# Adding the other experts' sums into PSUM by unit products, with a new order of the last units

## The chip, the cores and the metric

The kernel runs on one core of one Trainium2 chip. The metric is the device time of one execution in microseconds (us), the median of three runs. The engines are TensorE (PE; its weight loads are listed as PEld), VectorE (DVE), ScalarE (ACT), GpSimd (POOL) and SyncE (SP), which here only issues transfers.

## The reference

Two layers of a decoder trunk on 256 tokens of width 1024, all in f32. Each layer has a mixer (causal spatial gating beside latent attention) and a channel part. The channel part of the second layer is a top-2-of-8 mixture of SwiGLU experts, and the change lies at its end:

```python
h = rms_norm(x, norm_ffn_pre) * (1 + sc_f) + sh_f          # (256, 1024)
# for each token the two experts with the highest logits, gates = softmax of the two
y[token] = sum over its 2 experts e of gate * (silu(h @ w1[e]) * (h @ w3[e])) @ w2[e]
x = x + g_f * rms_norm(y, norm_ffn_post)                   # the output
```

Each expert has 3584 hidden columns; w1, w3 and w2 of all eight experts are 352 MB, and each is read once.

## The kernel before

**Units.** The expert stage is cut into 56 units (`UNITS`, from `SMALL_AT`): eight experts times `NG` = 7 groups of 512 hidden columns. A unit needs three pairs of weight chunks, 2 MB each (w1, w3, w2). Experts are sorted by their number of tokens. Four are *large* (up to 128 rows; each weight chunk is split by ACT and DVE into two f32r parts, and PE makes three products for each, lines 2177 to 2179). Four are *small* (64 rows, the expert `TINY` 32; PE multiplies the f32 chunk as it is, line 2692, with two or four products beside each other in the array). `SMALL_AT` says at which of the 56 places a unit of a small expert stands. The last expert is `END`, a small one: its units 3 to 6 are units 52 to 55.

**PE's order.** `unit(n)` does the w1 products of unit n, the transposes of unit n-1 (line 2734), the w3 products of unit n, and `unit_down(n-1)`, the w2 products of the unit before. After the loop come `unit_down(55)` and `last_scatter`. PE does all in this order.

**Weights.** SP issues the transfers in the order of use, into a ring of places; a transfer waits until PE has used what lay in its place. Pairs go as one transfer of 2 MB. Only the last pair, the w2 of unit 55 (`LAST_PAIR`), goes as two transfers of 1 MB with a semaphore each.

**Rows of the other experts.** When an expert other than `END` is finished (two units after its last one), ACT scales its rows by the gates and POOL writes them to a table in HBM by an indirect DMA (`scatter_rows`, line 864; its count is `rows_out`). When all are written (`ALL_ROWS`), POOL clears two buffers and gathers from the table, for each of the two blocks of 128 tokens, the first and the second choice (four indirect DMAs of 512 KB, line 896) into `y_exp` and `y_second`. DVE adds the two (line 2142).

**The end.** PE has the sums of `END` in bank 6. ACT copies them to `r5` (`last_y`, line 1338). `last_scatter` (line 2869) distributes the rows to the tokens by four products of 64 rows, one for each block t and half of the width (q = 2t + half), into the banks `DRAIN`. DVE adds each bank to `y_exp` (`add_y`, line 2025), ACT squares each half with its sum (`y_half`, line 1347), DVE and ACT make 1/rms (`y_inverse`, line 2123, and `root`, line 946), DVE multiplies by the gate row (`gated`, line 2129), scales and adds the residual (`last_residual`, line 2134), and SP stores four halves of 256 KB (line 702).

Of the kernel before, what the change touches and what calls it, by code (L numbers as in the profile page):

```python
# [223 lines left out]
def item_order():  # L224

    out = []
    for g in range(NG):
        out += [(spot(kind, g, 0), kind, g) for kind in ("w1", "w3")]
        if g:
# [3 lines left out]

LAST = [(PER_ITEM - 2, "w2", NG - 1)]
DRAIN = (7, 0, 1, 2)

LARGE = 5
HALF_CAP = P // 2
# [4 lines left out]
SMALL_ITEMS = (0, 5, TINY, 6)  # L243
LARGE_ITEMS = tuple(range(1, LARGE))
SMALL_AT = (0, 1, 2, 3, 4, 5, 6, 7, 8, 9, 11, 13, 16, 19,
            22, 25, 28, 31, 34, 37, 41, 44, 47, 49, 52, 53, 54, 55)


def units():
# [52 lines left out]
def up_width(n):  # L302
    return GRP * small_cap(UNITS[n][0]) // P
# [27 lines left out]
def build(nc, A, out):  # L331
    with ExitStack() as ctx:
# [3 lines left out]
        def sem(name):  # L336
            return ctx.enter_context(nc.semaphore(name))
# [161 lines left out]
        def raw_of(r, e=CH):  # L499
            slot = RING[r][0]  # L500
            if slot >= ONCE_AT:
                return (r3, r57)[slot - ONCE_AT][:, 0:e]
            if slot == HIDDEN_AT:
                return b_whole[1].rearrange("p k s -> p (k s)")[:, 0:e]
            if slot >= TURNED_AT:
                return hT_raw[slot - TURNED_AT][:, 0:e]
            if slot >= HIGH_AT:
                return hi_raw[:, slot - HIGH_AT, 0:e]
            return raw[:, row_of(slot), 0:e] if slot <= NRAW else r6[:, (slot - NRAW - 1) * CH:(slot - NRAW - 1) * CH + e]
# [87 lines left out]
        x0_dve = sem("x0_dve")  # L597
        ym_done, xh_done, hf_dve, hbt_full, rs_ready = (sem(n) for n in ("ym_done", "xh_done", "hf_dve", "hbt_full", "rs_ready"))
        rows_out, y_in, y_whole = sem("rows_out"), sem("y_in"), sem("y_whole")
        m_sm = sem("m_sm")  # L600
        rows_marked, y_cleared = sem("rows_marked"), sem("y_cleared")
        tiny_slots = sem("tiny_slots")
        small_ready, experts_ready, half_ready = sem("small_ready"), sem("experts_ready"), sem("half_ready")
# [8 lines left out]
        def _(sp):  # L612
# [53 lines left out]
            def moe_load(c, kind, e, g):  # L666
                src = A["moe_" + kind]
                src = src[e, g] if isinstance(e, int) else src[bass.ds(e, 1), g, :, :].rearrange("e p n -> p (e n)")
                if paired(c):
                    sp.wait_ge(used, NW + max(RING[NR + c + half][2] for half in range(2)) - NR + 1)  # L670
                    sp.dma_start(pair_of(NR + c), src).then_inc(raw_full[RING[NR + c][3]], 16)
                    return
                for half in range(2):
                    r = NR + c + half
                    slot_free(r)
                    sp.dma_start(raw_of(r), src[:, half * CH:(half + 1) * CH]).then_inc(raw_full[RING[r][3]], 16)

            expert = {0: 0}

# [16 lines left out]
            unit_loads(UNITS_ALL - 1, ("w2",))  # L696

            def store(n):
                for i, (t, half) in enumerate(((1, 0), (1, 1), (0, 0), (0, 1))):
                    sp.wait_ge(o_done, 4 * n + i + 1)  # L700
                    at = slice(half * 512, (half + 1) * 512)
                    sp.dma_start(out[0, t * P:(t + 1) * P, at], o_sb[:, t, at]).then_inc(out_done, 16)
# [14 lines left out]
        def _(pool):  # L717
# [160 lines left out]
            for n in range(UNITS_ALL):  # L878
                if n in FINISH_AT:
                    scatter_rows(FINISH_AT[n])  # L880
                if n == CLEAR_AT:
                    clear_rows(END)
                    wait_emptied(pool, LAST_IN[ONCE_AT + 1])
                    take_gate(3, gate_f, gate_f_in)
            pool.wait_ge(rows_out, ALL_ROWS)
            pool.wait_ge(m_gath, 2 * EXPERTS)
            wait_emptied(pool, LAST_IN[NRAW + 1])
            for t in range(T):
                pool.memset(y_second[t][:, :], 0.0).then_inc(y_cleared, 1)
            pool.memset(y_exp, 0.0).then_inc(y_cleared, 1)  # L890
            pool.wait_ge(rows_marked, 1)
            pool.wait_ge(y_cleared, T + 2)
            for t in range(T):
# [8 lines left out]
        def _(act):  # L902
# [443 lines left out]
            def y_half(q):  # L1346
                act.activation(scratch[:, q // 2, (q % 2) * 512:(q % 2 + 1) * 512], y_exp[:, q // 2, (q % 2) * 512:(q % 2 + 1) * 512],
                               ACT.Square, scale=D ** -0.5, accum_out=ms[:, q:q + 1]).then_inc(sq_done, 1)
# [5 lines left out]
            act.activation(warm[:, :], warm[:, :], ACT.Sqrt)  # L1354
            last_y()
            for q in range(4):
                act.wait_ge(m_acc, q + 1)
                y_half(q)
                if q % 2:
                    root(1, q // 2)  # L1360
            act.wait_ge(route_ready, 1)
# [14 lines left out]
        def _(dve):  # L1376
            steps = [0]

            def link(ins):

                steps[0] += 1
                ins.then_inc(v_step, 1)
                dve.wait_ge(v_step, steps[0])
# [635 lines left out]
            def add_y(i, q, bank=7):  # L2019

                ya = y_exp[:, q // 2, (q % 2) * 512:(q % 2 + 1) * 512]
                if q == 0 and i >= EXPERTS:
                    dve.wait_ge(m_acc, (i - (EXPERTS - 1)) * 4)
                dve.wait_ge(m_sc, (i - (EXPERTS - 1)) * 4 + q + 1)
                dve.tensor_tensor(ya, ya, ps[:, bank, :], ALU.add).then_inc(m_acc, 1)
# [102 lines left out]
            def gated(t):  # L2128
                return dve.tensor_tensor(y_sb[:, t, :], y_exp[:, t, :], gate_f[:, :], ALU.mult)
# [12 lines left out]
                dve.tensor_tensor(y_exp[:, t, :], y_exp[:, t, :], y_second[t][:, :], ALU.add).then_inc(y_whole, 1)  # L2142
            dve.wait_ge(y_whole, T)
            dve.wait_ge(gate_f_in, 16 * L)
            for q in range(3):
                add_y(EXPERTS - 1, q, DRAIN[q])
            y_inverse(0)
            add_y(EXPERTS - 1, 3, DRAIN[3])
            dve.wait_ge(m_acc, 4)
            gated(1)  # L2150
            y_inverse(1)
            link(gated(0))
            dve.wait_ge(rstd_ready, roots[0])
            last_residual(1)
            last_residual(0)
            spare = dve.value_load(info[0:1, ITEMS:ITEMS + 1], min_val=0, max_val=SPARE)
            with dve.If(spare > 0):
                dve.wait_ge(out_done, 64)
                for i in range(EXPERTS, ITEMS):
                    with dve.If(spare > i - EXPERTS):  # L2160
                        spare_item(i)
                        drain(i)
                dve.memset(small[:, 1:2], 0.0).then_inc(sum_ready, 1)
                gated(0)
                link(gated(1))
                y_inverse(0)
                y_inverse(1)
                dve.wait_ge(rstd_ready, roots[0])
                last_residual(1)
                last_residual(0)  # L2170


        @block.tensor
        def _(pe):
# [505 lines left out]
            def whole_part(c):  # L2680

                wait_full(pe, NR + c)
                return raw_of(NR + c)

            def part(i, c):
                return moe_part(i * PER_ITEM + c)

# [49 lines left out]
            def unit_down(n, turn_next=False):  # L2737
                i, g = UNITS[n]
                small = SMALL[n]
                if g == 0:  # L2740
                    before_ = same_kind_before(FINISH + [END], i)
                    if before_ is not None:
                        pe.wait_ge(m_yc, FINISHED[before_])
                    elif not small:
                        pe.wait_ge(idx_ready, 3)
                pe.wait_ge(m_h, n + 1)
                if small:
                    for half in range(2):
                        w = whole_part(unit_chunk(n, "w2", half))
                        for cc in range(2):  # L2750
                            cap, turned = small_cap(i), up_width(n) // P
                            c = 2 * half + cc
                            m = beside(6, D, cap, hT_small(n)[:, c % turned, c // turned * cap:(c // turned + 1) * cap], w, cc * D,
                                       g == 0 and c == 0, g == NG - 1 and c == 3)
                        m.then_inc(used, 1)
                        if turn_next and half == 0:
                            unit_turn(n + 1)
                    return
                for half in range(2):
                    wh, wl = moe_part(unit_chunk(n, "w2", half))  # L2760
                    for cc, q in itertools.product(range(2), range(2)):
                        c = 2 * half + cc
                        w = slice(cc * D + q * 512, cc * D + (q + 1) * 512)
                        first, final = g == 0 and c == 0, g == NG - 1 and c == 3
                        m = three(ps[:, 4 + q, :], bTh[:, c, 0:P], bTl[:, c, 0:P], wh[:, w], wl[:, w], first, final)
                    m.then_inc(used, 1)
                    if turn_next and half == 0:
                        unit_turn(n + 1)
# [95 lines left out]
            def last_scatter():  # L2864
                pe.wait_ge(m_gtc, 1)
                pe.wait_ge(m_yc, EXPERTS)
                for q in range(4):
                    at = slice(q % 2 * HALF_CAP, (q % 2 + 1) * HALF_CAP)
                    pe.matmul(ps[:, DRAIN[q], :], r4[at, 512 + q // 2 * P:512 + (q // 2 + 1) * P], r5[at, 0:512],
                              start=True, stop=True).then_inc(m_sc, 1)  # L2870

            for n in range(UNITS_ALL):
                unit(n)
            unit_down(UNITS_ALL - 1)
            last_scatter()
            pe.wait_ge(route_ready, 1)
# [94 lines left out]
```

## Time and profile before

| | |
|---|---|
| median of three runs | 1364.44 us (1363.46 to 1365.38) |
| the profiled execution | 1364.49 us |
| its span | 1362.8 us |
| outside the span | 1.69 us |
| PE busy | 1327.3 us, 97% |
| DVE, ACT busy | 903.3 us (66%), 675.1 us (50%) |
| read from HBM | 496.12 MB, 367 GB/s over the span |

Times in the text are counted from the start of the span. A row of the timeline gives the start, the duration, the engine, the line, what it writes and reads, the number of instructions merged, and in brackets the idle time before it and what ended it. Durations of PE's rows overlap, since products are pipelined; the distance between starts is what a product costs in a full queue. An f32 product stands as two records (line 2869 is four products and eight records).

### The profile page before, as it was taken

How to read it: one execution, taken by the hardware profiler on the slowest of the kernel's cores; microseconds unless marked ns; L12 is line 12 of the kernel's file. 1: busy time of each engine (PE TensorE's matmuls, PEld its weight loads, DVE VectorE, ACT ScalarE, POOL GpSimd, SP SyncE). 2: the span in 40 equal slices, each digit the busy share in tenths (PEclk: the TensorE clock that was granted, in tenths of full speed). 3: DMA queues.
4: the chain of work that ended last, by engine and by line, in shares of the span. 5: the costliest groups of instructions: out<-in, count | busy, mean ns of one | idle time of the engine just before them, and what ended most of it. 6: DMA issues, size and time to landing. Idle time of an engine off the chain costs nothing.

```text
span 1362.8 us, 19221 instructions
## 1 busy us (share of the span) xinstructions
PE 1327.3 (97%) x7925; PEld 1021.0 (75%) x7925; DVE 903.3 (66%) x1105; ACT 675.1 (50%) x773; POOL 60.0 (4%) x133
## 2 busy tenths in 40 slices
PE   9999999999999999999999999999998999999985
PEld 6788879878888888656677777777877887777752
DVE  6799979878778965200366765775767687676513
ACT  2783553534467643112355645565646576554501
POOL 6000000000000000100000000000000001000020
PEclk9999999999999999999999999999998999999998
DMA  9929939988654599899999999999999999999994
GB/s 367 418 107 351 390 111 397 422 314 347 236 203 163 194 385 407 335 421 423 425 428 427 428 428 399 428 427 427 427 428 426 427 427 427 428 427 427 427 427 192
DMA packets 52959, 500.59 MB, mean 367 GB/s; under 512 B 6272, under 2 KB 6400, under 8 KB 13058
## 3 DMA queue, kind: packets, MB, share of 16 engines
q1 hardware_dynamic: 50114, 490.90, 87.3%
q0 software_dynamic: 2752, 8.41, 1.7%
q8 instruction: 64, 1.05, 0.3%
q14 instruction: 29, 0.24, 0.0%
HBM read 496.12 MB, written 4.08 MB: 367 GB/s over the span
## 4 chain that ended last, share of the span: by engine, by line
PE 81%; DMA 9%; DVE 6%; ACT 2%; SPq 1%; issue 1%; DVEq 0%; ACTq 0%
PE ps L2177 20%; PE ps L2179 20%; PE ps L2178 19%; PE ps L2692 16%; DMA raw<-in_moe_w_dram 7%; PE ps L2671 2%; DMA raw<-in_w_first_dram 2%; PE ps L2734 1%; DVE lo L1454 1%; DVE lo L1482 1%; ACT hi L928 1%; ACT hi L911 1%; DVE raw L1395 1%; DVE mx L1688 0%; DVE r L1696 0%
## 5 line engine op out<-in xcount | busy, mean ns | idle before, releaser
L1482 DVE TENSOR_TENSOR lo<-raw,hi 128x2048 fp32r<-128x2048 f32 x136 | 308.6, 2287 | 174.7 <-ACT hi L928 174.6
L2177 PE MATMUL ps<-hi,hT_hi 128*128 128x512 f32 (+3 forms) x912 | 355.1, 389 | 4.2 <-DVE hT_lo L1508 1.9
L2179 PE MATMUL ps<-hi,hT_lo 128*128 128x512 f32 (+3 forms) x912 | 348.9, 383 | 0.0
L928 ACT ACTIVATE hi<-raw 128x2048 fp32r<-128x2048 f32 x136 | 256.0, 1913 | 158.0 <-DMA raw<-in_moe_w_dram 158.0
L2178 PE MATMUL ps<-lo,hT_hi 128*128 128x512 f32 (+3 forms) x776 | 295.6, 381 | 0.0
L2177 PEld LDWEIGHTS ps<-hi,hT_hi 128*128 128x128 f32 x912 | 171.3, 188 | 47.3 <-issue 13.0
L2179 PEld LDWEIGHTS ps<-hi,hT_lo 128*128 128x128 f32 x912 | 171.2, 188 | 32.6
L1454 DVE TENSOR_TENSOR lo<-raw,hi 128x2048 fp32r<-128x2048 f32 (+3 forms) x82 | 174.7, 2143 | 24.8 <-ACT hi L911 23.5
L2177 PE MATMUL ps<-hi,bT_hi 128*128 128x512 f32 (+2 forms) x416 | 166.0, 399 | 9.2 <-DVE bT_lo L1999 8.7
L2178 PEld LDWEIGHTS ps<-lo,hT_hi 128*128 128x128 f32 x776 | 145.8, 188 | 25.1
L2178 PE MATMUL ps<-lo,bT_hi 128*128 128x512 f32 (+2 forms) x416 | 162.6, 391 | 0.0
L2179 PE MATMUL ps<-hi,bT_lo 128*128 128x512 f32 (+2 forms) x416 | 162.3, 390 | 0.0
L911 ACT ACTIVATE hi<-raw 128x2048 fp32r<-128x2048 f32 (+3 forms) x82 | 145.3, 1802 | 30.0 <-DMA raw<-in_w_fu_dram 15.8
L2692 PE MATMUL ps<-raw,bT_first 128*32 128x128 f32 (+3 forms) x1456 | 124.6, 367 | 4.4 <-DMA raw<-in_moe_w_dram 4.4
L2692 PEld LDWEIGHTS ps<-raw,bT_first 128*32 128x32 f32 (+1 forms) x1456 | 62.0, 119 | 56.4 <-issue 41.8
L2177 PEld LDWEIGHTS ps<-hi,bT_hi 128*128 128x128 f32 (+1 forms) x416 | 79.0, 190 | 33.3 <-DVE bT_lo L1999 8.6
L1250 ACT ACTIVATE bT_first<-ps 128x256 f32<-128x256 f32 (+1 forms) x28 | 10.0, 357 | 177.0 <-PE ps L2734 177.0
L1395 DVE SCALAR_TENSOR_TENSOR raw<-raw,c_rows 128x1024 f32<-128x1024 f32 x80 | 94.6, 1219 | 0.1
L2179 PEld LDWEIGHTS ps<-hi,bT_lo 128*128 128x128 f32 (+1 forms) x416 | 79.2, 190 | 16.0
L2692 PE MATMUL ps<-raw,bT_second 128*64 128x256 f32 x752 | 87.8, 387 | 2.9 <-DMA raw<-in_moe_w_dram 2.9
L2178 PEld LDWEIGHTS ps<-lo,bT_hi 128*128 128x128 f32 (+1 forms) x416 | 79.3, 191 | 14.7
L2006 DVE TENSOR_TENSOR r<-r,ps 128x256 f32<-128x256 f32 (+1 forms) x28 | 10.7, 383 | 112.4 <-PE ps L2692 112.4
(384 smaller groups left out, 1266.3 us busy)
## 6 DMA issues: line engine op xcount, KB each, us to landing
raw<-in_moe_w_dram SPq DMA_DIRECT2D x116, 2048.0 KB, 17.2
r<-in_moe_w_dram SPq DMA_DIRECT2D x22, 2048.0 KB, 16.0
raw<-in_w_ada_dram SPq DMA_DIRECT2D x40, 1024.0 KB, 7.6
raw<-in_moe_w_dram SPq DMA_DIRECT2D x36, 1024.0 KB, 12.4
hi_raw<-in_moe_w_dram SPq DMA_DIRECT2D x13, 1024.0 KB, 11.1
raw<-in_w_fd_dram SPq DMA_DIRECT2D x11, 1024.0 KB, 8.3
raw<-in_w_ga_dram SPq DMA_DIRECT2D x8, 1024.0 KB, 6.9
raw<-in_w_gb_dram SPq DMA_DIRECT2D x8, 1024.0 KB, 6.8
```

Source lines behind the costliest of these rows:

```text
L911: act.activation(high_of(s, e), raw_of(r, e), ACT.Copy).then_inc(hi_done, 1)
L928: act.activation(high_of(s), raw_of(r), ACT.Copy).then_inc(hi_done, 1)
L1395: m = dve.scalar_tensor_tensor(w, w, 1.0, cbc[:, :], ALU.mult, ALU.mult, accum_out=av[:, k:k + 1])
L1454: dve.tensor_tensor(low_of(r, e), raw_of(r, e), high_of(s, e).bitcast(f32), ALU.subtract).then_inc(raw_done, 1)
L1482: dve.tensor_tensor(low_of(r), raw_of(r), high_of(s).bitcast(f32), ALU.subtract).then_inc(raw_done, 1)
L2006: dve.tensor_tensor(h_small[:, 0:w], h_small[:, 0:w], ps[:, 1, 0:w], ALU.mult).then_inc(m_sm, 1)
L2177: pe.matmul(o, wh, mh, start=first, stop=False)
L2178: pe.matmul(o, wh, ml, start=False, stop=False)
L2179: return pe.matmul(o, wl, mh, start=False, stop=last)
L2671: m = pe.matmul(ps[:, 3, kk * P:kk * P + width], x[:, t, k * P:(k + 1) * P], r4[:, t * P:t * P + width], start=(t == 0), stop=(t == T - 1))
L2692: m = pe.matmul(ps[q * cap:(q + 1) * cap, bank, 0:width], stationary, w[:, at + q * width:at + (q + 1) * width], start=first, stop=last)
L2734: m = pe.transpose(ps[:, 2, c * P:(c + 1) * P], src[:, c * P:(c + 1) * P], ident[:, :])
```

## The change

1. **Order of the units.** The last small places in `SMALL_AT` move: large units end at unit 49 instead of 51, so that units 46 to 49 are four large ones in a row, and units 50 to 55 are six small ones of `END`.
2. **POOL.** It no longer waits for all rows ahead of the clearing; the first buffer waits for nothing new, the second for the rows of `TINY`, and the wait for `ALL_ROWS` stands behind the clearing.
3. **Unit products.** DVE no longer adds the scattered banks to `y_exp`. Instead PE writes `y_exp` into the four banks `SUM_BANK` by products with the unit matrix `ident` (`first_sums`), between `unit(55)` and `unit_down(55)`, and `last_scatter` adds to these banks (`start=False`).
4. **The end.** ACT squares from the banks; DVE multiplies bank by gate half by half after each square, and goes through block 0 ahead of block 1.
5. **The last chunk.** Its 1 MB goes in two transfers of 512 KB; the first has a semaphore of its own (`last_half_in`), so that PE can use it ahead of the second.

```diff
+SUM_BANK = (3, 4, 5, 7)
...
 SMALL_AT = (0, 1, 2, 3, 4, 5, 6, 7, 8, 9, 11, 13, 16, 19,
-            22, 25, 28, 31, 34, 37, 41, 44, 47, 49, 52, 53, 54, 55)
+            22, 25, 28, 31, 34, 37, 41, 45, 50, 51, 52, 53, 54, 55)
...
                     slot_free(r)
-                    sp.dma_start(raw_of(r), src[:, half * CH:(half + 1) * CH]).then_inc(raw_full[RING[r][3]], 16)
+                    parts = 2 if c + half == LAST_PAIR + 1 else 1
+                    for q in range(parts):
+                        at, w = q * CH // parts, CH // parts
+                        landed = last_half_in if parts == 2 and q == 0 else raw_full[RING[r][3]]
+                        sp.dma_start(raw_of(r)[:, at:at + w], src[:, half * CH + at:half * CH + at + w]).then_inc(landed, 16)
...
-            pool.wait_ge(rows_out, ALL_ROWS)
             pool.wait_ge(m_gath, 2 * EXPERTS)
             wait_emptied(pool, LAST_IN[NRAW + 1])
             for t in range(T):
+                if t:
+                    pool.wait_ge(rows_out, ROWS_OUT[TINY])
                 pool.memset(y_second[t][:, :], 0.0).then_inc(y_cleared, 1)
             pool.memset(y_exp, 0.0).then_inc(y_cleared, 1)
+            pool.wait_ge(rows_out, ALL_ROWS)
...
             for q in range(4):
-                act.wait_ge(m_acc, q + 1)
-                y_half(q)
+                act.wait_ge(m_sc, q + 1)
+                act.activation(scratch[:, q // 2, (q % 2) * 512:(q % 2 + 1) * 512], ps[:, SUM_BANK[q], :],
+                               ACT.Square, scale=D ** -0.5, accum_out=ms[:, q:q + 1]).then_inc(sq_done, 1)
                 if q % 2:
                     root(1, q // 2)
...
-            for q in range(3):
-                add_y(EXPERTS - 1, q, DRAIN[q])
-            y_inverse(0)
-            add_y(EXPERTS - 1, 3, DRAIN[3])
-            dve.wait_ge(m_acc, 4)
-            gated(1)
-            y_inverse(1)
-            link(gated(0))
-            dve.wait_ge(rstd_ready, roots[0])
-            last_residual(1)
-            last_residual(0)
+            for t in range(T):
+                for half in range(2):
+                    q = 2 * t + half
+                    dve.wait_ge(sq_done, squares[0] + half + 1)
+                    m = dve.tensor_tensor(y_sb[:, t, half * 512:(half + 1) * 512], ps[:, SUM_BANK[q], :], gate_f[:, half * 512:(half + 1) * 512],
+                                          ALU.mult)
+                m.then_inc(y_whole, 1)
+                y_inverse(t)
+            dve.wait_ge(y_whole, 2 * T)
+            for t in range(T):
+                dve.wait_ge(rstd_ready, roots[0] - T + t + 1)
+                last_residual(t)
...
+                        last = unit_chunk(n, "w2", half) == LAST_PAIR + 1
+                        w = half_part(LAST_PAIR + 1) if last else whole_part(unit_chunk(n, "w2", half))
                         for cc in range(2):
+                            if last and cc:
+                                w = whole_part(LAST_PAIR + 1)
...
-                    pe.matmul(ps[:, DRAIN[q], :], r4[at, 512 + q // 2 * P:512 + (q // 2 + 1) * P], r5[at, 0:512],
-                              start=True, stop=True).then_inc(m_sc, 1)
+                    pe.matmul(ps[:, SUM_BANK[q], :], r4[at, 512 + q // 2 * P:512 + (q // 2 + 1) * P], r5[at, 0:512],
+                              start=False, stop=True).then_inc(m_sc, 1)
+
+            def first_sums():
+                pe.wait_ge(m_gtc, 1)
+                pe.wait_ge(m_yc, EXPERTS - 1)
+                pe.wait_ge(y_whole, T)
+                for q in range(4):
+                    pe.matmul(ps[:, SUM_BANK[q], :], ident[:, :], y_exp[:, q // 2, q % 2 * 512:(q % 2 + 1) * 512], start=True, stop=False)
 
             for n in range(UNITS_ALL):
                 unit(n)
+            first_sums()
             unit_down(UNITS_ALL - 1)
             last_scatter()
```

The order of the stores (block 0 first) and a branch that these inputs don't enter follow along.

## Rows read from the trace of the kernel before

**Rows 1.** The page: PE's busy time, share of the span, instructions.
```profile
PE 1327.3 (97%) x7925; PEld 1021.0 (75%) x7925; DVE 903.3 (66%) x1105; ACT 675.1 (50%) x773; POOL 60.0 (4%) x133
```
**Rows 2.** Stretches: PE, PEld, DVE, ACT, POOL busy; then PEclk, DMA share, GB/s.
```profile
1200.00:1300.00 100.00, 99.89 (x547) 73.05 (x546) 64.07 (x68) 47.90 (x38) 0.00 (x0) 1.00 1.01 428
...
1320.00:1337.00 17.00, 13.13 (x86) 7.45 (x84) 0.42 (x1) 0.66 (x2) 3.01 (x3) 0.90 1.00 419
1337.00:1347.00 10.00, 6.94 (x36) 2.17 (x34) 2.42 (x3) 1.87 (x3) 0.00 (x0) 1.00 0.48 199
```
**Rows 3.** Timeline of ACT: splits that waited for the next 2 MB of weights.
```profile
1191.81 3.72 ACT L928 ACTIVATE hi<-raw 128x2048 fp32r<-128x2048 f32 x2 [2.38 <-DMA raw<-in_moe_w_dram]
1196.71 3.72 ACT L928 ACTIVATE hi<-r 128x2048 fp32r<-128x2048 f32 x2 [1.18 <-DMA r<-in_moe_w_dram]
```
**Rows 4.** Timeline of PE, the last weights.
```profile
1321.90 3.65 PE L2692 MATMUL ps<-raw,bT_first 128*64 128x512 f32 x16 [1.31 <-DMA raw<-in_moe_w_dram]
...
1340.14 1.94 PE L2692 MATMUL ps<-raw,bT_first 128*64 128x512 f32 x8 [2.62 <-DMA raw<-in_moe_w_dram]
...
1342.38 3.65 PE L2692 MATMUL ps<-raw,bT_first 128*64 128x512 f32 x16
1346.47 1.94 PE L2692 MATMUL ps<-raw,bT_first 128*64 128x512 f32 x8 [0.45 <-DMA raw<-in_moe_w_dram]
```
**Rows 5.** Timeline of POOL: the last write of rows, the clearing, the first gather.
```profile
1303.66 0.96 POOL L864 DMA_INDIRECT rows_y<-r,choice_row  x1 [146.07 <-PE ps L2692]
1314.37 0.95 POOL L889 MEMSET c_rows<- 128x1024 f32 x1 [9.76 <-DMA rows_y<-r,choice_row]
...
1318.84 1.08 POOL L896 DMA_INDIRECT r<-rows_y,final_row  x1 [0.88 <-POOL r L890]
```
**Rows 6.** Timeline of DVE: the sum of both choices.
```profile
1345.01 1.23 DVE L2142 TENSOR_TENSOR r<-r,c_rows 128x1024 f32<-128x1024 f32 x1 [6.94 <-DMA gate_m<-rows_y,final_row]
```
**Rows 7.** Timeline of PE: f32 products of 512 columns, and the next row.
```profile
41.86 1.88 PE L2239 MATMUL ps<-gate_m,raw 128*128 128x512 f32 x4
43.58 2.42 PE L2239 MATMUL ps<-r,raw 128*128 128x384 f32 x8
```
**Rows 8.** Timeline of PE: f32r products of 512 columns, one record each.
```profile
1153.10 0.40 PE L2177 MATMUL ps<-hi,hT_hi 128*128 128x512 f32 x1
1153.33 0.39 PE L2178 MATMUL ps<-lo,hT_hi 128*128 128x512 f32 x1
```
**Rows 9.** Timeline: the scatter, the first sum, the first residual.
```profile
1349.26 1.99 PE L2869 MATMUL ps<-r 64*128 64x512 f32 x8 [0.85 <-ACT r L1338]
...
1350.49 1.88 DVE L2025 TENSOR_TENSOR r<-r,ps 128x512 f32<-128x512 f32 x3 [3.12 <-PE ps L2869]
...
1356.20 2.74 DVE L2134 SCALAR_TENSOR_TENSOR r<-raw,rstd,x_tok 128x512 f32<-128x512 f32 x4
```
**Rows 10.** Groups by line, 1330 to 1363 us: busy us, mean ns, idle before.
```profile
L2025 DVE TENSOR_TENSOR r<-r,ps 128x512 f32<-128x512 f32 x4 | 2.6, 680 | 3.1 <-PE ps L2869 3.1
L1347 ACT ACTIVATE r<-r 128x512 f32<-128x512 f32 x4 | 2.5, 617 | 2.1 <-DVE r L2025 2.1
...
L1347 ACT ACTIVATION_READ_ACCUMULATOR r<-r 128x1 f32 x4 | 0.7, 186 | 0.0
...
L946 ACT ACTIVATE rstd<-mean_sq 128x1 f32<-128x1 f32 x2 | 0.4, 202 | 1.1 <-DVE mean_sq L2125 1.1
...
L2125 DVE RECIPROCAL mean_sq<-mean_sq 128x1 f32<-128x1 f32 x2 | 0.3, 164 | 0.1
```
**Rows 11.** Timeline of PE: starts of units 43 (large), 44 and 46.
```profile
1152.29 0.50 PE L2177 MATMUL ps<-hi,hT_hi 128*128 128x512 f32 x1
...
1169.29 3.67 PE L2692 MATMUL ps<-raw,bT_second 128*64 128x256 f32 x32
...
1197.50 0.50 PE L2177 MATMUL ps<-hi,hT_hi 128*128 128x512 f32 x1
```
**Rows 12.** Weight transfers issued from 1100 to 1300: issue to landing.
```profile
DMA to landing us min/median/max: 12.5/17.7/19.8
```

More of the change, by code:

```diff
@@ L599, in build @@
         rows_out, y_in, y_whole = sem("rows_out"), sem("y_in"), sem("y_whole")
-        m_sm = sem("m_sm")
+        m_sm, last_half_in = sem("m_sm"), sem("last_half_in")
         rows_marked, y_cleared = sem("rows_marked"), sem("y_cleared")
@@ L698, in store @@
             def store(n):
-                for i, (t, half) in enumerate(((1, 0), (1, 1), (0, 0), (0, 1))):
+                for i, (t, half) in enumerate(((0, 0), (0, 1), (1, 0), (1, 1))):
                     sp.wait_ge(o_done, 4 * n + i + 1)
@@ L2158, in _ @@
                 dve.wait_ge(out_done, 64)
+                for q in range(4):
+                    dve.tensor_copy(y_exp[:, q // 2, (q % 2) * 512:(q % 2 + 1) * 512], ps[:, SUM_BANK[q], :]).then_inc(m_acc, 1)
                 for i in range(EXPERTS, ITEMS):
@@ L2168, in _ @@
                 dve.wait_ge(rstd_ready, roots[0])
+                last_residual(0)
                 last_residual(1)
-                last_residual(0)
         @block.tensor
@@ L2683, in whole_part, with half_part @@
                 return raw_of(NR + c)
+            def half_part(c):
+                pe.wait_ge(last_half_in, 16)
+                return raw_of(NR + c)
             def part(i, c):
@@ L2748, in unit_down @@
                     for half in range(2):
-                        w = whole_part(unit_chunk(n, "w2", half))
+                        last = unit_chunk(n, "w2", half) == LAST_PAIR + 1
+                        w = half_part(LAST_PAIR + 1) if last else whole_part(unit_chunk(n, "w2", half))
                         for cc in range(2):
+                            if last and cc:
+                                w = whole_part(LAST_PAIR + 1)
                             cap, turned = small_cap(i), up_width(n) // P
@@ L2868, in last_scatter @@
                     at = slice(q % 2 * HALF_CAP, (q % 2 + 1) * HALF_CAP)
-                    pe.matmul(ps[:, DRAIN[q], :], r4[at, 512 + q // 2 * P:512 + (q // 2 + 1) * P], r5[at, 0:512],
-                              start=True, stop=True).then_inc(m_sc, 1)
+                    pe.matmul(ps[:, SUM_BANK[q], :], r4[at, 512 + q // 2 * P:512 + (q // 2 + 1) * P], r5[at, 0:512],
[4 more added lines that the diff above has]
+                pe.wait_ge(y_whole, T)
+                for q in range(4):
+                    pe.matmul(ps[:, SUM_BANK[q], :], ident[:, :], y_exp[:, q // 2, q % 2 * 512:(q % 2 + 1) * 512], start=True, stop=False)
             for n in range(UNITS_ALL):
                 unit(n)
+            first_sums()
             unit_down(UNITS_ALL - 1)
```

## The prediction

> **What bounds the kernel now.** I read the page first: PE is busy for 97% of the span [rows 1], which says little here, since records of pipelined products overlap. The stretches say more. From 1200 to 1300 us the transfers have a DMA share of 1.01 at 428 GB/s, and still 1.00 at 419 GB/s from 1320 to 1337; only in the last ten microseconds of the stream does it fall to 0.48 [rows 2]. So the expert stage ends when the weights have come in. ACT's splits show the pace: each waited for a DMA, 4.90 us apart, which is one pair of chunks of 2 MB [rows 3]. Then I read the end of PE's timeline. The work on the last but one pair, w2 of unit 54, begins at 1340.14 after 2.62 us of waiting for it; from there PE works without a pause to 1346.03 (1342.38 + 3.65), waits only 0.45 us for the last chunk, and ends at 1348.41 [rows 4]. That is what the reader is to see: ahead of the last chunk PE has almost no spare time. From 1321.90 to 1346.47, four pairs, the pace is 6.14 us, not 4.90: the gathers run beside the weights there, from 1318.84 [rows 5] to 1345.01, where DVE's wait for the last of them ends [rows 6]. They cost the stream 24.57 - 4 x 4.90 = 4.97 us.
>
> After the last product the chain goes ACT copy, PE scatter at 1349.26, DVE add at 1350.49, squares, gate, and the first residual at 1356.20 [rows 9].
>
> **Edit 1 and 2, order and POOL.** Today POOL clears its buffers only when the last write of rows, issued at 1303.66, has landed, at 1314.37, and gathers from 1318.84 [rows 5]. With the large units done two places earlier that write comes about two units, some 29 us (six pairs of 4.90), earlier. The clearing then waits for the place of `y_exp`, which unit 52 still uses for its w3, so that the gathers begin near 1301 and land near 1327 (the 26 us that they take now, from rows 5 and 6). The bytes are the same and the transfers have no free time in which to hide them (1.01 to 1300, 1.00 to 1337 [rows 2]): the 4.97 us are paid earlier, and the end of the stream stays at 1346.47. But the last pairs then come at the undisturbed pace. w2 of unit 54 lands 4.90 ahead of the end, at 1341.57, instead of 1340.14: this step alone costs 1.43 us, as PE's work after that pair has no slack.
>
> Four large units in a row: a large unit after a large one takes 17.0 us on PE [rows 11] against 14.7 us for its three pairs, so PE falls back by 2.3 us in each. Now it begins unit 46 at 1197.50, 5.7 us after the split of its weights began at 1191.81 [rows 3, 11]; with unit 44 large and unit 45 small I make that 8, and after four large ones 15. What is late next is the issue of the transfer that takes the freed place. The worst pair, w2 of unit 48, whose products come a unit later, would be used up some 20 us after it landed; the next pair in its place is due six pairs, 29.4 us, after it, so that issue to landing falls to about 9.3 us, where the shortest now is 12.5 [rows 12]. A pair takes 4.90, so I take no gap in the stream; below I price one. The six small units then need less of PE than the weights take, and it catches up before unit 54.
>
> **Edit 3, the unit products.** Four f32 products of 512 columns on the whole array. The nearest row: two such products (four records) take 43.58 - 41.86 = 1.72 us, 0.86 each [rows 7]; four are 3.44 us. The lower bound is the price of f32r operands, 0.23 each [rows 8], 0.92 in all; the upper the row's full 1.88 for two, 3.8. `ident` and `y_exp` are f32, so I take 3.44. They stand in PE's order behind all of unit 55, `unit_down(54)` included, and ahead of `unit_down(55)`. The 2.62 us in which PE waits lie ahead of that place [rows 4] and can't cover them; behind it there are 0.45. What queues behind them is the last down product, and ACT's copy and the scatter wait for that. Their own wait for DVE's sum costs nothing: gathers that land at 1327 let DVE add in about 1341 to 1343.5, right behind its part of unit 55, while PE reaches the products near 1346.
>
> The Trainium skill, page "TensorE: Matmul & The Clock Gate", part "Wait — 56ns, not 53.3ns?", has bf16 products of 512 columns starting 215.7 ns apart. If that held here the four would be 0.86 us and the forecast 2.6 us lower; the f32 row above, four times as long, speaks against it.
>
> **Edit 5, the last chunk in two.** PE now does the chunk in 1.94 us after it lands. Alone, the split could hide half, 0.97. But PE arrives late: 1341.57 + 5.89 + 3.44 = 1350.9, when all of the chunk has lain there for 4 us. So I take 0, and 0.97 as the bound on the side of a gain.
>
> **Edit 4, the end**, counted from the start of the scatter. Now the first residual starts at 6.94 [rows 9]. After: banks ready at 1.23 as for DVE today; two squares of 0.62 and a read of 0.19 [rows 10] are done at 2.04 and 2.66; DVE multiplies (0.68 each, the add's duration) to 2.72 and 3.40; two small operations of 0.16 and their links bring 3.76; ACT, which stands in its order at the root (0.20), is free at 4.0. Squares 3 and 4 are done at 4.8 and 5.4, the products at 6.2, the small operations at 6.5, and the first residual starts: 0.45 earlier. The chain keeps its length because a read and a product of half a block now follow each square, in place of the four adds that go. Bounds: between 0 and a gain of 0.9, if records overlap as the three adds do (1.88 for three of 0.68).
>
> **The sum.** PE's work from the last but one pair: 5.89 + 1.94 = 7.83 now, 11.27 with the unit products. 1341.57 + 11.27 = 1352.84 against 1348.41: 4.43 later. Less 0.45: +3.98. The profiled execution took 1364.49 us, 0.05 over the median, so 1368.4 us.
>
> **The rivals.**
> *The pair lands as now.* If the gathers still end late, the pair keeps its 1340.14 and only the products count: 3.44 - 0.45 of idle - 0.45 = +2.5, 1367.0. For it: unit 52's use of the place. Against: 1301 is far from 1341.
> *The stream ends earlier*, the mechanism that ends on the other side: if the gathers, moved among units that PE bounds, find free transfer time, the stream loses up to 4.97 us less. Then 3.98 - 4.97 = -1.0, 1363.5; it is faster than now from 4 us on. Against it: a DMA share of 1.01 before 1300 [rows 2].
> *The unit products are covered*, as the change would have it: PE would have to wait 3.44 us for the last chunk. Then only edits 4 and 5 count, -0.97 - 0.45 = -1.4, 1363.1. Against: 0.45 us of idle.
> *The products are cheap* (0.92): +1.5, 1365.9.
> *The stream starves* in the four large units: a gap of 2 to 3 us goes straight to the end, 1371.
>
> **How the numbers follow.** Under 0.2%, 2.7 us, a difference of this kernel can't be told from none. Forecast 0.57, of which 0.05 fall under 2.7, since it lies only 1.3 above; pair as now 0.16, 0.07 of it over; early stream 0.08; covered 0.03; cheap 0.04; starved 0.08; something else that gains more than 2.7 us 0.04. Slower: 0.52 + 0.07 + 0.08 = 0.67; faster 0.04; same the other 0.29. The range leaves out the early stream, the cover and the unnamed gain, 0.15 together: it reaches from 1364.5 (cheap products, pair as now, 0.92 - 0.45 - 0.45) to 1371.4 (starved).
>
> **What would show it.** Right: eight records of `first_sums` lasting about 3.4 us between two stretches of line 2692; no idle of PE between them and the scatter beyond ACT's copy; last waits of PE for DMA 4.9 us apart; gathers issued near 1301; the scatter starting near 1353.7. Wrong: a wait of PE for weights behind the unit products, a stream that ends before 1345, or DMA share under 0.95 between 1240 and 1300.

## The result and the profile after

The changed kernel takes 1368.57 us (median of 7 runs, 1367.13 to 1369.8), beside 1364.72 us for the kernel before (7 runs): a ratio of 1.003, interval 1.002 to 1.004. The forecast was 1368.4 us, slower. The profiled execution took 1368.34 us with a span of 1366.6, which is 3.8 us over the span before. One run of the kernel before (1903.56 us) and one of the last kernel below (3442.02 us) lay far above all others and stand in none of the medians.

First the stretches of the changed kernel, with the columns of [rows 2]:

```profile
1240.00:1300.00 60.00, 60.00 (x371) 41.53 (x371) 25.54 (x34) 19.62 (x19) 4.54 (x4) 1.00 1.00 418
1320.00:1337.00 17.00, 11.42 (x84) 6.35 (x84) 0.42 (x1) 1.32 (x4) 0.00 (x0) 1.00 1.01 427
1337.00:1347.00 10.00, 8.64 (x52) 3.91 (x53) 2.69 (x3) 1.87 (x3) 0.00 (x0) 1.00 0.61 252
1347.00:1352.00 5.00, 5.00 (x19) 1.81 (x19) 0.00 (x0) 0.00 (x0) 0.00 (x0) 1.00 0.00 0
```
The transfers are full until 1337 as before (a share of 1.00 and 1.01), now undisturbed at 427 GB/s from 1320 where there were 419 [rows 2]. But from 1347 to 1352 PE is busy for all of 5.00 us while the DMA share is 0.00: the weights are in, and PE still works. The loss lies there: in the kernel before, the down products had ended at 1348.41 [rows 4]. The timeline of PE says with what it is busy:

```profile
1336.95 3.67 PE L2708 MATMUL ps<-raw,bT_second 128*64 128x256 f32 x32 [0.76 <-DMA raw<-in_moe_w_dram]
1341.98 1.94 PE L2708 MATMUL ps<-raw,bT_first 128*64 128x512 f32 x8 [1.35 <-DMA raw<-in_moe_w_dram]
...
1344.22 1.94 PE L2708 MATMUL ps<-raw,bT_first 128*64 128x512 f32 x8
1346.09 3.70 PE L2896 MATMUL ps<-r,ident 128*128 128x512 f32 x8
1349.72 3.65 PE L2708 MATMUL ps<-raw,bT_first 128*64 128x512 f32 x16
1354.22 1.99 PE L2888 MATMUL ps<-r 64*128 64x512 f32 x8 [0.85 <-ACT r L1345]
```
The answer to [rows 4]: the last-but-one pair is used at 1341.98 (1340.14 before), the four unit products (line 2896, eight records) hold PE for 3.63 us (1349.72 - 1346.09), and the last down product no longer waits for anything; in the trace its last quarters had landed at 1345.53 and 1346.77. The down products end at 1353.37 (1349.72 + 3.65), 4.96 us after the 1348.41 of before.

POOL and DVE, the answers to [rows 5] and [rows 6]:

```profile
1295.54 0.95 POOL L895 MEMSET c_rows<- 128x1024 f32 x1 [14.18 <-PE ps L2708]
...
1300.03 1.08 POOL L903 DMA_INDIRECT r<-rows_y,final_row  x1 [0.91 <-POOL r L896]
```
```profile
1341.08 1.22 DVE L2150 TENSOR_TENSOR r<-r,c_rows 128x1024 f32<-128x1024 f32 x1
1342.22 1.22 DVE L2150 TENSOR_TENSOR r<-r,gate_m 128x1024 f32<-128x1024 f32 x1
```
The gathers begin 18.8 us earlier, and DVE's sums no longer wait for them. They end at 1343.4, 2.7 us before PE wants them.

The end, the answer to [rows 9]:

```profile
1355.35 0.60 ACT L1365 ACTIVATE r<-ps 128x512 f32<-128x512 f32 x1 [1.27 <-PE ps L2888]
...
1356.17 1.29 DVE L2157 TENSOR_TENSOR raw<-ps,r 128x512 f32<-128x512 f32 x2 [12.73 <-ACT r L1365]
...
1360.04 2.74 DVE L2142 SCALAR_TENSOR_TENSOR r<-raw,rstd,x_tok 128x512 f32<-128x512 f32 x4
```
The first residual starts 5.82 us after the scatter (1360.04 - 1354.22) where it took 6.94. So 4.96 - 1.12 = 3.84, the 3.8 us of the span.

### The profile page after: what moved, and what is told of

Same layout as the page of the kernel before. It is cut to its first block, busy times and chain, and to the rows that moved or that the text cites. A ratio compares the mean times of both kernels' runs of the same rounds, so it can differ in the third digit from the quotient of the medians.

```text
span 1366.6 us, 19239 instructions
## 1 busy us (share of the span) xinstructions
PE 1330.1 (97%) x7933; PEld 1023.4 (75%) x7933; DVE 901.3 (66%) x1103; ACT 674.5 (49%) x773; POOL 59.3 (4%) x133
## 4 chain that ended last, share of the span: by engine, by line
PE 86%; DMA 6%; DVE 5%; ACT 2%; issue 1%; DVEq 0%; POOL 0%; SPq 0%; ACTq 0%; POOLq 0%
PE ps L2188 20%; PE ps L2190 20%; PE ps L2189 20%; PE ps L2708 16%; DMA raw<-in_moe_w_dram 6%; PE ps L2250 2%; PE ps L2682 2%; PE ps L2750 1%; DVE lo L1462 1%; DVE lo L1490 1%; DVE raw L1403 1%; ACT hi L935 0%; DVE mx L1696 0%; DVE r L1704 0%; ACT hi L918 0%
```

## The experiments

The theory: the unit products stand on the path at full length, the new order adds about 1 us, the end gives back about 1 us. The rivals: the order alone costs it all; the place or the waits of the products cost, and not their length; the last transfer rather than the pair before it sets the end. The table has for each kernel its median less that of the kernel before in the same job, and from its one profile two lengths that don't depend on where the stream of weights stood in that execution: from the landing of the last weights to the start of the scatter, and from there to the end of the span (good to about 0.05 us, since the span is given in tenths).

| kernel | against before, us | weights in to scatter | scatter to end |
|---|---|---|---|
| before | | 2.83 | 13.54 |
| changed | +3.85 | 7.45 | 12.38 |
| no_products, no_products_again | +0.09, +0.68 | 3.68, 3.63 | 12.57, 12.58 |
| short_products | +1.36 | 4.95 | 12.44 |
| order_alone | +0.67 | 3.72 | 13.53 |
| order_late_gathers | -0.51 | 3.22 | 13.53 |
| old_order | +4.59 | 8.31 | 12.85 |
| one_last_transfer | +3.75 | 7.47 | 12.58 |
| halves_alone | +2.46 | 6.67 | 12.40 |
| sums_in_gaps | +1.44 | 3.66 | 12.59 |
| sums_in_gaps_head | +2.31 | 4.84 | 12.60 |
| gaps_and_halves | -0.57 | 2.15 | 12.40 |
| early_sums | +3.86 | 7.51 | 12.55 |

**Without the products.**

```diff
-            first_sums()
             unit_down(UNITS_ALL - 1)
```
(and `start=True` in `last_scatter`).

> The changed kernel without the four unit products; the scatter opens the PSUM sums itself, so the output lacks the sums of the other experts. All waits and the order stay. Theory (products are exposed): the last down product starts as soon as the one before it ends, 3.63 us earlier (1349.72 - 1346.09 in the changed kernel's profile), unless the last quarters land after that; they landed at 1345.53 and 1346.77, so the start is at about 1346.1 to 1346.8 and the time 1368.6 - 3.6 = 1365.0, at the least 1368.6 - 2.9 = 1365.7. Rival (products run in time that TensorE would wait anyway): 1368.6, no change.

It took 1365.18 us, ratio 0.9999 (0.999 to 1.0008).

```profile
1341.37 1.94 PE L2708 MATMUL ps<-raw,bT_first 128*64 128x512 f32 x8 [1.35 <-DMA raw<-in_moe_w_dram]
...
1343.61 5.37 PE L2708 MATMUL ps<-raw,bT_first 128*64 128x512 f32 x24
1349.83 1.99 PE L2888 MATMUL ps<-r 64*128 64x512 f32 x8 [0.85 <-ACT r L1345]
```
The same chain with the gap closed: 24 records in a row. The loss is gone with the products.

**Short products.**

```diff
+            dve.tensor_copy(ident_r[:, :], ident[:, :]).then_inc(y_whole, 1)
-  pe.matmul(ps[:, SUM_BANK[q], :], ident[:, :], y_exp[:, q // 2, q % 2 * 512:(q % 2 + 1) * 512], start=True, stop=False)
+  pe.matmul(ps[:, SUM_BANK[q], :], ident_r[:, :], y_round[:, q // 2, q % 2 * 512:(q % 2 + 1) * 512], start=True, stop=False)
```


> The changed kernel, but VectorE writes the sums of the other experts, and a copy of the unit matrix, as f32r, so that the four products are f32r products (the sums are rounded on the way, the rest stays f32). An f32r product of 512 columns took 0.23 us in the kernel before, one in f32 0.91. Theory (the whole length of the products stands on the path): four take 0.92 instead of 3.63 us, time 1368.6 - 2.7 = 1365.9. Rival (their place or their waits cost, and their length does not): 1368.6.

It took 1365.87 us, ratio 1.0009 (1.0 to 1.0018).

```profile
1346.63 1.19 PE L2899 MATMUL ps<-y_round,ident_r 128*128 128x512 f32 x4
1347.76 3.65 PE L2711 MATMUL ps<-raw,bT_first 128*64 128x512 f32 x16
```
Same place, same waits, 1.13 us instead of 3.63, and 2.5 us less in both measures (7.45 to 4.95; +3.85 to +1.36). So length is what costs. With the run before this settles the main step.

**The order alone, and the order with late gathers.** Both are the kernel before with edits 1 and 2; the second has one wait more:

```diff
             wait_emptied(pool, LAST_IN[NRAW + 1])
+            pool.wait_ge(used, NW + unit_chunk(UNITS_ALL - 2, "w1", 1) + 1)
```


> The kernel before with only the new order of units and the earlier clearing, so gathers as early as in the changed kernel; tail as before. Theory (the gathers now lie before the last weights and push the last-but-one pair back): the pair is used about 1342.0 instead of 1340.1, later work keeps its length, time 1364.7 + 1.4 to 1.9 = 1366.1 to 1366.6. Rival (the order is free, all of the loss is the products'): 1364.7.

> The order alone, but GpSimd clears only after TensorE has used the w1 of unit 54, so that the gathers start at about 1319 to 1322, near the kernel before (1318.84). Theory (the gathers' place sets when the pair lands): the pair lands at about 1340.1 again, time 1364.7; if the gathers now delay the last quarters, up to 1366. Rival (the order itself, six small units in a row, sets it): the same as the order alone, 1366.1 to 1366.6.

They took 1365.76 us, ratio 1.0003 (0.9994 to 1.0012), and 1364.58, ratio 0.9997 (0.9988 to 1.0006). Neither is told from the kernel before. The traces say more; first the order alone:

```profile
1340.81 1.94 PE L2694 MATMUL ps<-raw,bT_first 128*64 128x512 f32 x8 [1.35 <-DMA raw<-in_moe_w_dram]
1342.68 0.44 PE L2736 MATMUL ps<-ident,r 128*128 128x128 f32 x2
1343.05 5.37 PE L2694 MATMUL ps<-raw,bT_first 128*64 128x512 f32 x24
```
and with late gathers:

```profile
1340.17 3.48 PE L2695 MATMUL ps<-raw,bT_first 128*64 128x512 f32 x8 [2.61 <-DMA raw<-in_moe_w_dram]
1343.58 0.44 PE L2737 MATMUL ps<-ident,r 128*128 128x128 f32 x2
1343.95 5.37 PE L2695 MATMUL ps<-raw,bT_first 128*64 128x512 f32 x24
```
In the first, the pair landed 4.87 us ahead of the last weights (1340.68 and 1345.55), in the second 6.91 (1340.04 and 1346.95); before it was 6.43. So the place of the gathers moves the pair, as forecast, and weights to scatter grows by 0.89. My expectation for the order alone was too high, since it counted the pair's delay in full; PE's 0.45 us of waiting for the last chunk [rows 4] takes up part of it, as the prediction's own sum (4.43 - 3.44 = 1.0) had it. In the second trace the eight records took 3.48 us instead of 1.94: the granted clock was 0.54 from 1340 to 1343.6. Without these 1.54 us PE would again have waited for the last chunk, so the 0.39 us by which weights to scatter (3.22) lies above the kernel before (2.83) can be put down to the clock and not to the order.

**The old order.** `SMALL_AT` as before, the rest as changed.

> The changed kernel with the order of units of the kernel before. Theory: gathers are issued near 1318 again and land late; VectorE's second sum ends near 1346.2 to 1347.4, TensorE's products wait for it, then 3.6 us of products and 3.7 + 3.7 us of down work: scatter at about 1354.5 to 1355.5, time 1368.8 to 1369.9. Rival (the order costs the 1.4 to 1.9 us and the products find the gap): 1366.7 to 1367.2.

It took 1369.68 us, ratio 1.0032 (1.002 to 1.0044).

```profile
1347.05 3.67 PE L2896 MATMUL ps<-r,ident 128*128 128x512 f32 x8 [2.05 <-DVE r L2150]
```
With late gathers the products wait 2.05 us for DVE's sum: once the products are there, the new order is worth about 0.7 us (+4.59 against +3.85), though the two intervals overlap.

**The last chunk in one transfer.**

```diff
-                    parts = 2 if c + half == LAST_PAIR + 1 else 1
+                    parts = 1
```


> The changed kernel with the last chunk in one transfer of 1 MB. Theory (TensorE comes to the last chunk 2.95 us after it has landed, 1349.72 - 1346.77, so that the split is worth nothing): 1368.6, within 0.5. Rival (the split lets TensorE start a quarter earlier): 1.0 us longer, 1369.6.

It took 1368.26 us, ratio 1.0033 (1.002 to 1.0046), and 7.47 us from weights to scatter beside 7.45. The split is worth nothing here.

**Two pairs in halves.** `first_in` holds a semaphore for the first half of the pairs w3 of unit 55 and w2 of unit 54.

```diff
+        if c in first_in:
+            for half, landed in enumerate((first_in[c], raw_full[RING[NR + c][3]])):
+                at = slice(half * CH, (half + 1) * CH)
+                sp.dma_start(pair_of(NR + c)[:, at], src[:, at]).then_inc(landed, 16)
+            return
```


> The changed kernel, products where the change put them, with one edit: the pairs w3 of unit 55 and w2 of unit 54 come in two transfers of 1 MB each, with a semaphore each. Theory (the chain that ends the stage starts when weights of the last-but-one pair are there, and the products lie in it): the first half lands 2.4 us earlier, TensorE's work from there on is the same 11.3 us, the second half (1341.9) and the last quarters (1345.5, 1346.8) are in time, so that down products end 2.3 us earlier, 1366.3. Rival (the last transfer of the stream sets the end, not this pair): 1368.6.

It took 1366.85 us, ratio 1.0018 (1.0009 to 1.0027): about 1.4 us less than the changed kernel, not 2.3.

```profile
1332.15 5.36 PE L2717 MATMUL ps<-raw,bT_second 128*64 128x256 f32 x32 [2.05 <-DMA raw<-in_moe_w_dram]
...
1337.81 3.67 PE L2717 MATMUL ps<-raw,bT_second 128*64 128x256 f32 x32
1341.31 1.89 PE L2717 MATMUL ps<-raw,bT_first 128*64 128x512 f32 x8
```
The first half of the pair landed at 1339.47, as reckoned, but PE came to it at 1341.31: w1 of unit 55 had taken 5.36 us instead of 3.67. The stretches show the clock:

```profile
1332.00:1337.50 5.50, 5.35 (x33) 3.76 (x34) 0.00 (x0) 0.00 (x0) 0.00 (x0) 0.69 1.02 425
1337.50:1341.00 3.50, 3.50 (x33) 2.32 (x34) 0.00 (x0) 0.66 (x2) 0.00 (x0) 1.00 1.00 413
```
The pair does start the chain that ends the stage; what the halves give is partly lost to 1.69 us (5.36 - 3.67) of half clock that no wait for weights absorbs any more. For the other runs of this kernel that is not shown.

**The products in PE's waits.** Each block's sum waits for its own gathers alone, and the products go into units 54 and 55:

```diff
+                if n == UNITS_ALL - 1:
+                    first_sums(1)
                 unit_up(n, "w3")
+                if n == UNITS_ALL - 2:
+                    first_sums(0)
```


> The changed kernel with the same four products, but the sum of each block of tokens waits only for its own two gathers; the two products of block 0 stand before the down products of unit 53, inside unit 54, and the two of block 1 inside unit 55, ahead of its w3 products. Theory (only the place of the products costs): TensorE waits there for weights, 2.60 us and 0.76 + 1.35 us in the changed kernel, so that 1.8 us of products in each stretch are covered; down products end about 3.6 us earlier, 1365.0. Rival (the products delay the freeing of the weights' places or hold up the transposes, so the weights come later): 1366.5 to 1368.6.

It took 1365.95 us, ratio 1.001 (1.0001 to 1.0018).

```profile
1325.39 1.98 PE L2901 MATMUL ps<-r,ident 128*128 128x512 f32 x4
1328.03 3.65 PE L2709 MATMUL ps<-raw,bT_first 128*64 128x512 f32 x16 [0.65 <-DMA raw<-in_moe_w_dram]
...
1337.72 1.88 PE L2901 MATMUL ps<-r,ident 128*128 128x512 f32 x4
...
1343.66 1.94 PE L2709 MATMUL ps<-raw,bT_first 128*64 128x512 f32 x8 [0.45 <-DMA raw<-in_moe_w_dram]
```
PE still waits for the weights behind both groups, 0.65 and 0.45 us: the products are covered, and weights to scatter is 3.66, as without products. Yet the runs are 0.8 to 1.4 us above those without products, though the intervals overlap. Three more runs look for that.

> The products in the gaps, with those of block 1 at the head of unit 55 instead of ahead of its w3 products. Theory (in either place they run while TensorE would wait for weights, and the 1.3 us by which the first form was above the kernel without products were the spread of where the stream stands): the same as the kernel without products that runs beside it, within 0.7. Rival (the products ahead of w3 delayed the end): the first form's 1366 less about 0.9; or, if any product in the gaps delays the stream, again 1.3 us above the kernel without products.

> The changed kernel without the four unit products once more (the output lacks the sums of the other experts), beside the two others on one chip, as the floor of what hiding the products can give: 3.6 us below the changed kernel, about 1365.0.

1366.7 us, ratio 1.0015 (1.0006 to 1.0024), beside 1365.07, ratio 1.0003 (0.9994 to 1.0013). The first expectation missed by 1.6 us, and the first trace has a reason that I had not seen:

```profile
1331.88 3.53 PE L2901 MATMUL ps<-r,ident 128*128 128x512 f32 x4 [2.21 <-DVE r L2079]
1335.35 3.74 PE L2709 MATMUL ps<-raw,bT_second 128*64 128x256 f32 x32
```
At the head of unit 55 the products wait 2.21 us for the sum, as the last gather landed at 1330.49, and then run at a granted clock of 0.55 (1331.8 to 1335.3). PE comes late to the next weights.

The third takes the sums early on DVE and leaves the products where the change put them.

> The changed kernel with the products where the change put them, but VectorE's sums as in the kernels with products in the gaps: each block's sum at the head of units 54 and 55, on a semaphore of its own. Those three kernels took 1.2 to 1.5 us more, against the kernel before, than last weights to scatter and scatter to end account for in their profiles. Theory (the products on TensorE inside units 54 and 55 cost that): 3.9 us above the kernel before, as the changed kernel. Rival (the early sums, with VectorE's waits inside the units, cost it): 5.1 to 5.3 us above.

1368.39 us, ratio 1.003 (1.002 to 1.0041), as the changed kernel: the early sums cost nothing that these runs show. What is left as a cause are the products inside units 54 and 55, in a way that the profile of one execution doesn't show, or chance (see what stays open).

**Products in the waits, with halves and earlier gathers.** The products of block 1 at the head of unit 55, both pairs in halves, and `y_second` cleared ahead of POOL's wait for the place of `y_exp`.

> As the products in the gaps, with three more edits: the products of block 1 stand at the head of unit 55, where TensorE waited 1.88 us; GpSimd clears one buffer before its last wait, so that the gathers start up to 1.8 us earlier; and the pairs w3 of unit 55 and w2 of unit 54 come in two transfers of 1 MB each with a semaphore each, so that TensorE can start on the first half. Theory (now the last pair's landing sets the end): the first half of the pair w2 of unit 54 is used about 1.2 to 2.4 us earlier, down products end at 1347.8 to 1348.4, and the shorter tail makes 1363.0 to 1363.6, faster than the kernel before. Rival (what lands last stays at 1346.8 and all work after it keeps its length, or the smaller transfers run slower): 1364.5 to 1365.0.

It took 1363.94 us, ratio 0.9997 (0.9988 to 1.0006).

```profile
1331.67 1.98 PE L2910 MATMUL ps<-r,ident 128*128 128x512 f32 x4
...
1341.06 1.89 PE L2718 MATMUL ps<-raw,bT_first 128*64 128x512 f32 x8
...
1345.71 3.65 PE L2718 MATMUL ps<-raw,bT_first 128*64 128x512 f32 x16 [0.53 <-DMA raw<-in_moe_w_dram]
```
PE waits for weights again at the very end (0.53, for the first half of the last pair), weights to scatter is 2.15 us, the shortest of all, and the gather was in time. By the table it should gain 16.37 - 14.55 = 1.82 us on the kernel before; the runs give 0.57, which isn't told from zero. It beats the changed kernel by over 4 us.

## Why the prediction was right

**The bound.** Right: the stage ends with the weights, and PE has almost no spare time from the last-but-one pair on. All kernels fit that, with the exception below.

**Order and POOL.** The gathers began at 1300.03 (forecast 1301) and the last landed at 1330.8 (1327): they took 30.8 us and not the 26 of the kernel before, which cost nothing here, since DVE came to their sums only at 1341. The stream ended at 1346.77 (1346.47), the pair was used at 1341.98 (1341.57), so both were later by 0.3 to 0.4. That the cost of the gathers is only moved holds: the stream ended no earlier in this trace. The net of this step, 1.0 us, stands beside 0.89 (order alone, weights to scatter) and 0.67 ± 1.2 in its runs. The large units gave no gap: the shortest issue to landing was 10.2 us (9.3 forecast).

**The products.** 3.63 us for 3.44: the records start 0.43 us apart (half of 0.86), and the rest is the change from and to the neighbours. Nothing covered them. Without them the runs are 3.2 to 3.8 us shorter, and with 1.13 us of products 2.5 us. The rival that they are cheap was wrong for f32 operands and about right for f32r ones (1.13 us for 0.92); that its 1365.9 meets the 1365.87 of the short products is helped by the two errors named below under "The end", which cancel there too. The Trainium skill, page "TensorE: Matmul & The Clock Gate", part "Wait — 56ns, not 53.3ns?", has back-to-back products of this width 215.7 ns apart at 2.4 GHz; the f32r ones here were 0.28 us apart (1.13 / 4), the f32 ones 0.91.

**The split.** Worth 0, as forecast (7.47 against 7.45).

**The end.** The term that was mis-sized: 1.12 us gained, where 0.45 was forecast and 0.9 was the bound. My sum laid ACT's squares, their reads and DVE's products end to end; in the trace the squares start 0.59 us apart, the read of one beside the next. The first square starts 0.10 us ahead of my sum (1.13 for 1.23 after the scatter), the second is done 0.27 ahead (2.39 for 2.66), the fourth 0.51 (4.89 for 5.4), and the residual starts 0.68 ahead (5.82 for 6.5). The two errors, 0.53 too little on PE (4.96 for 4.43: 0.41 from the pair's later use, 0.12 from the work behind it) and 0.67 too little gained, cancelled. The mechanism was right; that the number came within 0.2 us is in good part luck.

**What stays open.** The three kernels with products inside units 54 and 55 took 1.2 to 1.6 us more than the table's lengths account for (1.44 against -0.12, 2.31 against 1.07, -0.57 against -1.82); the others agree within 0.9. Each of the three is hardly more than the interval of its runs (1.2 us to either side), so it is their common direction that asks for a cause. One rival is that such products hold up the stream of weights. The profiles don't show it: from the landing of the pair thirteen places ahead of the last-but-one to the last landing the stream took 75.90, 75.71 and 76.60 us in these three, and 75.2 to 76.5 in the other eleven. Products that run while the clock is low, as in one of these traces, would do it in some executions. For it: the eleven runs of the first two spread over 4.5 and 3.8 us, those of the other edited kernels over 2.7 at most. Against it: the third spreads over no more than these (2.5). Only profiles of more executions could show it; the cause stays open.

## What to carry to other kernels

When a stage ends with its transfers, reckon from the last transfer that PE has to wait for: any work behind it is paid in full, but for what waits are left there, however idle PE was ahead of it. Moving work off the chain behind a stage is worth only what it shortens there (1.1 us), and its price at the new place must fall into a wait; look for one of its length and for what has to be ready by then. If no such wait is left, first make the work shorter (f32r operands, which round the sums, 1.13 us for 3.63) or let PE start on half a transfer.

## What the runs showed of the hardware

In thirteen of the fourteen profiles a group of products between 1310 and 1345 (with both pairs in halves, two) ran while the clock granted to PE was at its lower level (1.2 of 2.4 GHz); in the three shown above PE had just waited 2.05, 2.61 and 2.21 us, and the group took 5.36 us for 3.67, 3.48 for 1.94 and 3.53 for 1.98. Not every such wait does it: in the kernel before, PE waited 2.62 us ahead of 1340.14 [rows 4] and the clock stayed at 1.00 [rows 2]. The fall of that kernel lies earlier, on the w1 of unit 55:

```profile
1327.75 5.36 PE L2692 MATMUL ps<-raw,bT_second 128*64 128x256 f32 x32 [2.20 <-DMA raw<-in_moe_w_dram]
...
1333.85 3.67 PE L2692 MATMUL ps<-raw,bT_second 128*64 128x256 f32 x32 [0.37 <-DMA raw<-in_moe_w_dram]
```
PE still waits 0.37 us for the next weights, so this fall cost nothing. As long as a wait for weights follows, a fall is free; an edit that fills the waits takes this cover away.

The last weights landed between 1345.55 and 1348.45 us in fourteen profiles, and the spread is there well ahead of the edits: the pair thirteen places ahead of the last-but-one landed at 1270.32 in the changed kernel and at 1272.55 with the sums in the gaps, whose first moved sum begins at 1319.97. Lengths from the last landing on are what single profiles can compare.
